# A fused two-block network on one core: the passage into the state-space stage done by row tiles

## The reference, cut to what matters

```
x  = layer_norm(alpha * x + cat2 @ w_out_odd, ln_g[1], ln_b[1])   # end of the first part
hn = rmsnorm(x, norm_mix_w_2)                                     # begin of the second block
q, k, v, z, xbc, dt_raw = split(hn @ w_in_2)                      # 512, 512, 512, 1024, 1536, 16 columns
att = chunk_band_attention(q, k, v, rel_bias_2)
ssd = ssd_mixer(z, xbc, dt_raw, ...)       # conv over tokens, silu, time steps by softplus, chunked scan,
                                           # gate by silu(z), a group rms norm
x  = x + concatenate([att, ssd]) @ w_out_2
```

## Time and profile before

| | |
|---|---|
| median of 3 runs | 820.15 us (818.93 to 821.26) |
| the profiled execution | 820.23 us |
| its span in the trace | 818.4 us |
| PE busy | 797.9 us, 97% of the span |
| DVE busy | 514.6 us, 63% |
| ACT busy | 409.9 us, 50% |
| POOL busy | 98.3 us, 12% |

### The profile page before, as it was taken

The page is one execution under the profiler, slowest core; times in us unless marked ns, Lnnn a source line. Parts: engine busy times, 40 slices in busy tenths (PEclk is TensorE's granted clock), DMA queues, the critical chain, the costliest instruction groups (busy, mean ns, idle before and its releaser), DMA issues.

```text
span 818.4 us, 12972 instructions
## 1 busy us (share of the span) xinstructions
PE 797.9 (97%) x5044; PEld 698.8 (85%) x5044; DVE 514.6 (63%) x802; ACT 409.9 (50%) x599; POOL 98.3 (12%) x67
## 2 busy tenths in 40 slices
PE   8999999999999999999999899999998999999996
PEld 7998877799978878998787799799776999999995
DVE  6975556755656556567774745876755755555555
ACT  5534544454655533446663348465654544444441
POOL 2331000010100012111301227300000000000002
PEclk9999999999999999999999999999999999999999
DMA  9855544344755534755814255634216566556541
GB/s 329 303 192 182 195 155 154 106 134 117 238 200 155 202 106 144 242 182 181 257 43 142 72 188 159 202 106 152 98 45 218 182 208 204 175 187 201 168 146 51
DMA packets 75771, 137.43 MB, mean 168 GB/s; under 512 B 7104, under 2 KB 13504, under 8 KB 75712
## 3 DMA queue, kind: packets, MB, share of 16 engines
q1 hardware_dynamic: 74464, 132.15, 50.5%
q0 software_dynamic: 1248, 4.46, 1.7%
HBM read 132.80 MB, written 1.05 MB: 164 GB/s over the span
## 4 chain that ended last, share of the span: by engine, by line
PE 88%; DVE 5%; issue 2%; ACT 1%; DMA 1%; POOL 1%; SPq 0%; POOLq 0%; DVEq 0%; ACTq 0%
PE acc L951 13%; PE acc L953 13%; PE acc L952 13%; PE acc L959 12%; PE acc L961 12%; PE acc L960 12%; DVE w_lo L680 1%; PE acc L1168 1%; PE acc L1202 1%; DMA raw<-in_w_in_even 1%; PE acc L1152 1%; PE acc L1032 1%; PE acc L1141 1%; PE acc L1081 1%; PE acc L1046 1%
## 5 line engine op out<-in xcount | busy, mean ns | idle before, releaser
L680 DVE TENSOR_TENSOR w_lo<-raw,w_hi 128x1024 fp32r<-128x1024 f32 (+1 forms) x228 | 277.7, 1232 | 194.6 <-ACT w_hi L660 101.0
L959 PE MATMUL acc<-x_hi,w_hi 128*128 128x256 f32 x840 | 241.0, 287 | 2.1 <-DVE w_lo L680 1.2
L961 PE MATMUL acc<-x_hi,w_lo 128*128 128x256 f32 x840 | 237.7, 283 | 0.0
L960 PE MATMUL acc<-x_lo,w_hi 128*128 128x256 f32 x840 | 237.7, 283 | 0.0
L660 ACT ACTIVATE w_hi<-raw 128x1024 fp32r<-128x1024 f32 (+1 forms) x133 | 136.9, 1030 | 140.4 <-PE acc L961 77.2
L650 ACT ACTIVATE w_hi<-raw 128x1024 fp32r<-128x1024 f32 x112 | 119.1, 1063 | 132.3 <-PE acc L961 57.9
L959 PEld LDWEIGHTS acc<-x_hi,w_hi 128*128 128x128 f32 x840 | 160.9, 192 | 6.0 <-issue 3.2
L960 PEld LDWEIGHTS acc<-x_lo,w_hi 128*128 128x128 f32 x840 | 160.8, 191 | 1.1 <-issue 0.7
L961 PEld LDWEIGHTS acc<-x_hi,w_lo 128*128 128x128 f32 x840 | 160.8, 191 | 0.0
L951 PE MATMUL acc<-w_hi,cat_hi 128*128 128x512 f32 x296 | 118.9, 402 | 2.7 <-issue 2.6
L953 PE MATMUL acc<-w_hi,cat_lo 128*128 128x512 f32 x296 | 116.2, 393 | 0.0
(11 more groups left out here) (259 smaller groups left out, 839.8 us busy)
## 6 DMA issues: line engine op xcount, KB each, us to landing
raw<-in_w_ff SPq DMA_DIRECT2D x32, 1024.0 KB, 5.3
raw<-in_w_in_even SPq DMA_DIRECT2D x28, 1024.0 KB, 5.1
raw<-in_w_in_odd SPq DMA_DIRECT2D x16, 1024.0 KB, 5.6
raw<-in_w_in SPq DMA_DIRECT2D x16, 1024.0 KB, 5.5
raw<-in_w_out_even SPq DMA_DIRECT2D x12, 1024.0 KB, 5.2
raw<-in_w_out SPq DMA_DIRECT2D x4, 1024.0 KB, 5.0
raw<-in_w_in_even SPq DMA_DIRECT2D x4, 512.0 KB, 6.7
raw<-in_w_ukv_even SPq DMA_DIRECT2D x8, 256.0 KB, 3.3
```

Of the source, the lines that this page charges most:

```text
L680: ins = eng.tensor_tensor(lo, r, hi.bitcast(F32), ALU.subtract)
L959: pe.matmul(o, wh[:, k, fs], hi[:, ka, :], start=start and f % 2 == 0, stop=False, skip_group_check=True)
L960: pe.matmul(o, wh[:, k, fs], lo[:, ka, :], start=False, stop=False, skip_group_check=True)
L961: ins = pe.matmul(o, wl[:, k, fs], hi[:, ka, :], start=False, stop=stop, skip_group_check=True)
```

## The change

1. The last two k-tiles of `w_out_odd` become two pieces with both tiles kept in one slot, one for each chunk of 512 columns. They are multiplied row tile by row tile (`rows_of`): row tile 0 for both chunks first, then row tile 1.
2. Layer norm and rms norm run by row tile (`mix_rows`, `mix_turn`). PE's constant products are 13 ahead of the first tile's transposes and 3 between the tiles, in place of 24 and 3. The transposes are 8 a tile, `x_hi` and `x_lo` tiles are 128 columns wide. All squares and scalings are ACT's, in halves of 512 columns.
3. Half of the values (256 columns of v, all 8 k-tiles, one piece of 1 MB) is prepared early into the room of R3 (`v_hi`, `v_lo`), at the step `wide_weights` within the last attention unit. It is multiplied token-major for row tile 0 right after that tile's transposes, then the time-step product of that tile, then both for row tile 1.
4. The conv inputs follow. The steps of the conv and of z are reordered: `conv_end 1` after `conv 4`, and `conv_end 2` ahead of z's epilogue.
5. z's second chunk, q, k and the other half of v are cut into halves, with the scan's steps in the middle of a piece and not behind it. The other half of v is one piece of 8 k-tiles, its two halves around `ssd_turn`.

The core of the diff:

```diff
-BUSY = {("rms_norm", 0): (24, 3)}
+BUSY_MIX = (13, 3)
...
-    for m in range(2):
-        moba_out(7, m, 1)
-        step("epi", ys2[m])
-    step("layer_norm", 1)
-    step("rms_norm", 0)
+    for t in range(T):
+        for p in rows_pieces["out"]:
+            step("rows_of", (p, t, 1 - t, 2))
+    for c in ys2:
+        step("epi", c)
+    step("mix_rows", rows_pieces["out"])
+    for t in range(T):
+        step("mix_turn", t)
+        step("rows_of", (rows_pieces["v"], t, 0, 8))
+        step("rows_of", (rows_pieces["dt"], t, 0, 8))
+    step("mix_end", rows_pieces["dt"].n + 2)
...
-    parts += halves_of(lambda: chunk("tok", "x", NCOL, "copy_tok", dst=("R3", NCOL, 2048)), w["w_in_2"], SV)
-    for f, sts in zip(parts, between):
-        f()
...
+    def second_v():
+        c = chunk("tok", "x", NCOL // 2, "copy_tok", dst=("R3", NCOL, 2048 + NCOL // 2))
+        load(c, w["w_in_2"], 0, 8, SV + NCOL // 2, NCOL // 2)
+        step("epi", c)
+
+    parts[0]()
+    step("conv", 5)
+    parts[1]()
+    z_end = steps.pop()
+    step("conv_end", 2)
+    steps.append(z_end)
+    step("ssd_cums", 0)
+    between = [[("ssd_cb", 0), ("ssd_xs", 0), ("ssd_xs", 1)], [("ssd_rows", 0)], [("ssd_rows", 1)], [("ssd_rows", 2)], [("ssd_rows", 3)],
+               [("ssd_last", 0), ("ssd_gate", 0)], [("ssd_turn", 0)]]
+    for f, sts in zip(parts[2:] + [second_v], between):
+        one, two = by_halves(f)
+        one()
         for st in sts:
             step(*st)
+        two()
...
+            def mix_turn(t):
+
+                if t:
+                    keep_busy(aux[:, 3, :], BUSY_MIX[1])
+                rows = tmp[:, t * D:(t + 1) * D]
+                for h in range(2):
+                    pe.wait_ge(*due("mix_scaled", 2 * t + h + 1))
+                    for k in range(4 * h, 4 * h + 4):
+                        ins = pe.transpose(aux[:, 2 * t + h, (k % 4) * P:(k % 4 + 1) * P], rows[:, k * P:(k + 1) * P], ident)
+                    own(ins, "mix_turned")
...
+                elif kind == "mix_rows":
+                    last_out = i
+                    dve.wait_ge(*due("rows_done", 2))
+                    dve.wait_ge(*due("mix_used", 1))
+                    row_add(0, 0)
+                    dve.wait_ge(*due("mix_used", 2))
+                    row_add(1, 0)
+                    row_centred(0)
+                    row_normed(0)
+                    dve.wait_ge(*due("piece_used", last_out[0].n + 1))
+                    row_add(0, 1)
+                    row_mean_square(0)
+                    dve.wait_ge(*due("piece_used", last_out[1].n + 1))
+                    row_add(1, 1)
+                    row_centred(1)
+                    row_lo(0)
+                    row_normed(1)
+                    low_prep(dt_piece.n)
+                    row_mean_square(1)
+                    low_prep(conv_piece.n)
+                    row_lo(1)
```

More of the change, by code:

```diff
@@ L125, in __init__ @@
         self.off = 0
+        self.home = None
 class Chunk:
@@ L334, in moba_out, with apart, last_pieces, first_of_last @@
         load(ys2[n], w["w_out_odd"], k0, nk, n * NCOL)
+    def apart(make):
+        make()
+        return steps.pop()[1]
+    rows_pieces = {}
+    def last_pieces():
+        rows_pieces["sides"] = [pieces[-1]]
+        rows_pieces["out"] = [apart(lambda m=m: moba_out(6, m, 2)) for m in range(2)]
+        c = chunk("tok", "x", NCOL // 2, "copy_tok", dst=("R3", NCOL, 2048))
+        rows_pieces["v"] = apart(lambda: load(c, w["w_in_2"], 0, 8, SV, NCOL // 2))
+        c = chunk("tok", "x", SSD_HEADS, "copy_dt")
+        rows_pieces["dt"] = apart(lambda: load(c, w["w_in_2"], 0, 8, SDT, SSD_HEADS, order="beside"))
+        home = rows_pieces["sides"][0].n - 1
+        rows_pieces["sides"][0].home, rows_pieces["sides"][0].off = home % 2, HALF
+        for m, p in enumerate(rows_pieces["out"]):
+            p.home, p.off = (home + 1) % 2, m * HALF
+        rows_pieces["v"].home = "R3"
+        rows_pieces["dt"].off = 2 * HALF - rows_pieces["dt"].room
+        step("wide_weights", rows_pieces["v"])
+    def first_of_last():
+        for p in rows_pieces["out"]:
+            step("rows_of", (p, 0, 0, 1))
     whole_ones = moba_part(0, 1) + moba_part(1, 1)
@@ L346, in plan @@
             between[n + i] = [f]
-    for n, m in ((17, 0), (18, 1)):
-        between[n] = [lambda m=m: moba_out(4, m, 2)]
-    between[19] = [lambda m=m: moba_out(6, m, 1) for m in range(2)]
+    between[17] = [lambda: moba_out(4, 0, 2)]
+    between[18] = [lambda: moba_out(4, 1, 2), last_pieces]
+    between[19] = [first_of_last]
     pipeline(8, MOBA_HEADS, 2, between)
-    for m in range(2):
-        moba_out(7, m, 1)
-        step("epi", ys2[m])
-    step("layer_norm", 1)
-    step("rms_norm", 0)
+    for t in range(T):
+        for p in rows_pieces["out"]:
+            step("rows_of", (p, t, 1 - t, 2))
[7 more added lines that the diff above has]
+    step("mix_end", rows_pieces["dt"].n + 2)
+    c_dt = rows_pieces["dt"].chunk
+    step("epi", rows_pieces["v"].chunk)
+    step("dt_copy", c_dt)
     for n in range(3):
@@ L369, in plan @@
             step("conv", 2 * (n - 1) + 1)
[L370 to L379, removed]
+        if n == 1:
+            step("conv_end", 0)
+        if n == 2:
+            step("conv", 4)
+            step("conv_end", 1)
     parts = []
@@ L486, in build @@
         R2 = sb("R2", [P, 4096])
+        with nc.sbuf_tensor("v_hi", [P, 2 * HALF], F32R) as v_hi, nc.sbuf_tensor("v_lo", [P, 2 * HALF], F32R) as v_lo:
+            pass
         R3 = sb("R3", [P, 4096])
@@ L610, in pool_share @@
             if p.chunk.epilogue == "conv_in":
-                return {0: 2, 4: 0, 8: 4}[p.chunk.info["dst"]]
+                return {0: 0, 4: 0, 8: 4}[p.chunk.info["dst"]]
             if p in by_rows:
@@ L631, in slot_free @@
             at = (0, HALF) if half else (HALF, 2 * HALF) if p.nk == 4 else (p.off, p.off + p.room)
-            for m in range(n - 2, -1, -2):
+            for m in range(n - 1, -1, -1):
                 q = pieces[m]
-                if at[0] < q.off + q.room and q.off < at[1]:
+                if q.home == p.home and at[0] < q.off + q.room and q.off < at[1]:
                     if q.nk == 4 and at[1] <= HALF:
@@ L684, in build @@
             before = pieces[p.n - 2]
-            if p.room <= HALF and before.off + before.room <= HALF:
+            if p.room <= HALF and p.off == 0 and before.home == p.home == p.n % 2 and before.off + before.room <= HALF:
                 p.off = HALF
@@ L881, in product @@
                         pe.wait_ge(*due("acc_read_" + before.reader, before.read_count))
-                if c.acts == "x" and not p.turn_after and p.n >= 2 and p.n not in AFTER_MIX:
+                if c.acts == "x" and not p.turn_after and p.n >= 2:
                     x_ready(p.k0 + p.nk)
-                products_of(p, range(2 if part == 0 else p.nk))
+                products_of(p, range(p.nk // 2 if part == 0 else p.nk))
             def heads_ready(c, k0, k_last):
```

279 lines of the change are left out of this document (167 added, 112 removed).

## The result

| | before | after |
|---|---|---|
| median | 819.81 us (818.93 to 821.26, 4 runs) | 830.43 us (829.4 to 832.08, 4 runs) |
| the profiled execution | 820.23 us | 832.08 us |
| its span | 818.4 us | 830.3 us |

The ratio is 1.0129, with a 95% interval of 1.0115 to 1.0142: the change costs 10.6 us. The profiled execution is the longest of its four; against that of before it is 11.9 us longer.

What follows compares the result with a forecast made beforehand. PE was taken as the bound (88% of the chain). 7.3 - 7.55 + 1.9 - 0.5 + 0.4 + 5.65 = +7.2, plus 1.5 for the clock, on 820.23 gave 828.9, or 828.8 against the median; range 820.5 to 832.

Steps and rivals of the forecast that it cites:

- the passage at full clock: From the last output product to the first conv product: the latter comes at 473.3, 7.3 us later than 466.00.
- work taken off later: After the passage, the time-step product (2.27) and half of v (5.28) go: 7.55 us off.
- the clock: PE's clock may fall at three holes, up to 1.5 us each; one fall was taken, +1.5.
- The turn: Ahead of scores 24: `cat_hi` and `cat_lo` queue behind a weight copy that waits for all of v, +5.65 us.
- The passage pays itself back: Passage lengthening against work removed later: 7.3 for 7.55, paid back to within 0.3 us.
- The wait ahead of `ssd_cb`: State-space stage: a 5.4 us chain against 3.5 us of PE work gives a new wait of 1.9 us.
- The gate: At `ssd_gate`, a subtraction of 1.23 stands ahead; PE waits about 1.15 instead of 0.78, +0.4 us.
- The copy of v queued behind the blocked weight copy: Ahead of the first conv product, which needs v copied out of PSUM: 1.06 + 0.5 us with hand-overs.
- the hidden turn: Rival: the wait in the turn is hidden anyway, its price about 4 lower; 821.5 to 823 us; chance 0.13.
- the shorter passage: Rival: first conv product at 470.5, total 826; faster than before only with the turn's wait hidden too; chance 0.1.
- The clock in each hole: Rival: the clock falls in all three holes, +4.5 us, total 832; chance 0.19.
- The values did fill the holes: Passage: values fill the holes; the rival, values only after both tiles' transposes, costs 3 more, 832; chance 0.03.

Runs made afterwards that it cites:

- experiment 1: Changed kernel, with ACT's copy and DVE's subtraction for the next `w_out_2` half piece moved behind the turned tiles: 822.09 us, 1.003 to before.
- experiment 3: Changed kernel, with 4 more constant products behind each tile's transposes and 5, not 3, ahead of the second tile's: 829.09 us, 1.0103 to before.
- experiment 7: The kernel of 6 with the tanh of `conv_end 2` earlier on ACT: 818.97 us, 0.9985; then also z's epilogue behind the small copies: 816.89 us, 0.997.
- experiment 2: Changed kernel, with 12 constant products in PE's wait ahead of scores 24, the wait itself kept: 828.18 us, 1.0097 to before.
- 8: Experiment 7's first kernel, v's early half prepared behind the gated heads: 819.61 us, 0.9994; its second, that half's low part on POOL: 816.61 us, 0.9959.
- 5: Changed kernel, with z's third piece whole ahead of `ssd_cb`, not cut into halves around it: 833.95 us, 1.0163 to before.
- the kernel of 6: Changed kernel with the edits of experiment 1 and experiment 3, and v's copy out of PSUM ahead of the blocked weight copy: 819.14 us, 0.9987.

## Why the prediction was right, point by point

The forecast was slower, 828.8 us; measured were 830.4. The mechanism is as forecast, and one term, the clock, was sized too small. The 11.9 us of the profiled execution add up like this, with the forecast in brackets: the last k-tile's product 0.1 late (0), the passage at full clock 7.5 (7.3), work taken off later -7.7 (-7.55), waits 1.62 - 0.47 + 0.16 + 5.65 = 7.0 (7.45), the clock 2.0 in the passage, 2.0 behind scores 24 and 1.0 at a hole near the end (1.5 for all of it).

- **The turn.** Forecast +5.65 for the wait ahead of scores 24. The trace has 5.65, where there was none, and experiment 1 shows the cause: the same kernel with the turned tiles ahead of the blocked copy has no wait. That ACT's queue lets nothing pass is now seen in a row: 6.73 us at the weight copy, with `cat_hi` behind it at once, although the transposes had been over for 3 us. The Trainium skill (PSUM — Partial Sum Buffer, "Engine vs sequencer instructions") says that ScalarE and VectorE take their queues strictly first in, first out; by that row the rule holds here.
- **The passage at full clock.** Forecast: first conv product at 473.3. It came at 475.61. The constants began at 449.37 for 449.05, the transposes at 455.33 for 455.25, tile 0's values at 458.47 for 458.25. The chain of DVE, ACT and POOL was sized to within 0.3 us up to there; eight copies of 128 columns took 2.16 on DVE, 0.27 each, as put. In experiment 3, where no clock fell, the first conv product came 28.45 behind the last k-tile's (472.36 for 443.91); the forecast was 473.3 for 444.8, 28.5.
- **The passage pays itself back.** At full clock, yes. By experiment 3 it costs 28.45 for the 20.97 of before, 7.5. From the first conv product to scores 24 it took 114.67, before 115.43, so -0.8, and with 7.0 of new waits in it the work taken off is 7.7. But at the clock that it got, the passage cost 9.5.
- **The wait ahead of `ssd_cb`.** Forecast 1.9; measured 1.62 (the 0.24 behind it was there before, and the 0.47 ahead of the last products went, as forecast). The place and the direction were right, the size 0.3 too high. Of the two things named in the chain, the tanh behind the weight copy gave only 0.2 of the wait by itself in experiment 7; with z's epilogue behind the small copies as well, the wait was gone.
- **The gate.** +0.4 forecast, +0.16 measured (0.94 for 0.78).
- **The clock** is the term that was mis-sized. The step was "not every one needs to come, so I take one, +1.5". All three came: 1.3 and 1.5 us in the tiles' values, of which 2.0 reached the first conv product (30.45 for 28.45), and 2.0 behind scores 24, by the trace and by experiment 2. So 4.0 for 1.5. And a fourth came, which the forecast had no term for, at the hole of 2.0 us near the end of the band attention that both kernels have, in this execution and not in that of before (0.75 over the 6.7 us from 633.3). It cost 1.0, and by the other traces of this study it comes in some executions and not in others (last section). That the falls in the values are the holes' doing is shown by experiment 3, and that behind scores 24 by experiment 2.
- **At the end of the products before the passage.** PE's wait of 1.83 at the last k-tile was not named as a wait, though its end was placed to within 0.4 (445.16 for 444.8). The copy of v queued behind the blocked weight copy was in the sum (1.06 + 0.5), and came as 1.66.

The rivals: the hidden turn and the shorter passage didn't happen. The clock in each hole did: its price was 4.5 for three falls, they took 4.0, and its 832 was the profiled execution's time. The median lay between it and the forecast. The values did fill the holes in part.

There is some luck in the total. The clock term was 3.5 short in the profiled execution, and that execution is the longest of the four, 1.65 us above the median. That the forecast lies 1.6 from the median says less for it than the single terms do.

What stays open: how many of the falls the other executions had, and whether POOL's share in 8 is a gain in the whole time.

## What to carry to other kernels

In an engine that takes its work in one order, a preparation for later work that has to wait is free only as long as nothing that PE waits for stands behind it. When a piece is made larger or moved behind another step, look up what its slot's release now waits for, and what is queued behind that wait. Here one weight copy, with its subtraction, placed ahead of the turned tiles cost some 8 of 10.6 us; by the traces 5.6 of wait and 2.0 of lower clock behind it. And when work is put into a seam to fill it, count the holes that are left: three edits that changed nothing of the work, only its order and constants in the holes, turned a loss of 10.6 us into a gain of 1.1, and two more into one of 2.5.

## What the runs showed of the hardware

A fall of the clock isn't tied to a place. The norm done by row tiles near 306 us is the same in both kernels, with the same holes of 0.92 and 1.13 us. In the execution of before it was followed by products of 0.63, in that of after by products of 0.39 to 0.40:

```profile
309.32 0.39 PE L1034 MATMUL acc<-w_lo,x_hi 128*128 128x512 f32 x1
...
314.21 1.09 PE L1107 MATMUL acc<-cst,res 128*128 128x128 f32 x8 [1.33 <-DVE res L1707]
```

And there the fall cost nothing: at full clock PE waits 1.33 us for DVE ahead of the next transposes, which start at 314.21; at the lower clock they started at 314.35 with no wait. Here the lower clock cost nothing since the time was spent waiting anyway. Of the twelve profiled executions of this study two fell in this place, before and experiment 1.

Near the end the same play has a price. At the hole of 2.0 us that all twelve have at the end of the band attention, six fell (after, experiments 1 and 5, the kernel of 6 and both of 8) and six did not. From the product behind that hole to the end of the span it takes 194.8 to 195.0 us in the first six and 193.9 to 194.0 in the others: 1.0 us that comes in some executions and not in others, with the same products in that place. Before is one of the six without, but it has only this one execution with a trace.
